# All weight matrices laid out by load on the host, one contiguous piece per partition

## What is computed

```python
def first_block(x, ...):
    p = rmsnorm(x) @ w_in                                  # 1024 x 4128
    y = concat(gated_delta_rule(...), mlstm(...))          # scans in both directions
    x = x + y @ w_out
    x = x + peer(rmsnorm(x), peer_wq, peer_keys, peer_u, peer_v)
    return rmsnorm(x)

def peer(t, ...):                                          # 256 tokens, 8 heads, 16 rows each
    idx, gate = top16_of(t @ peer_wq, peer_keys)           # row numbers below 16384
    act = gelu(einsum("td,thkd->thk", t, peer_u[idx]))     # 256 * 128 rows of 4 KB
    return einsum("thk,thkd->td", gate * act, peer_v[idx]) # as many again

def second_block(x, ctx, ada_w, pool_w, attn_w_qkv, attn_w_o, ffn_w_up, ffn_w_down, ...):
    # two layers: shift, scale and gate from ada_w (2 x 1024 x 6144); layer 0 mixes by
    # windowed means and pool_w, layer 1 by attention; each ends in
    #   (silu(a) * v) @ w_down   with   a, v = split(conv3(h @ w_up))   # 1024 x 5632, 2816 x 1024
    # layer 0 is also worked out for ctx (256 tokens), whose keys and values layer 1 reads
```

## Time and profile before

| what | us |
|---|---|
| median of 3 runs | 2010.51 |
| lowest and highest | 2008.73 and 2012.59 |
| the profiled execution | 2012.46 |
| its span | 2010.6 |
| PE / PEld / DVE busy | 1535.4 / 1126.8 / 1066.7 |
| ACT / POOL busy | 530.5 / 800.6 |
| DMA, mean | 237 GB/s, 475.83 MB |

### The profile page before, as it was taken

One profiled execution on the slowest core, in us unless ns is written; L12 is line 12 of the kernel. 1 busy time (PEld: TensorE's weight loads), 2 busy tenths in 40 slices (PEclk: granted clock), 3 DMA queues, 4 the chain that ended last, 5 costly groups with the idle time before them and its releaser, 6 DMA issues.

```text
span 2010.6 us, 22323 instructions
## 1 busy us (share of the span) xinstructions
PE 1535.4 (76%) x8566; PEld 1126.8 (56%) x8566; DVE 1066.7 (53%) x2051; ACT 530.5 (26%) x757; POOL 800.6 (40%) x750
## 2 busy tenths in 40 slices
PE   7958889797122849988787577775998968779988
PEld 6736556566111737754343111114998966569988
DVE  1353343439999887775666300016775334547743
ACT  3222211112221222210002000015654342546532
POOL 0004230007746446557777666642553001005530
PEclk9978999899555869989998799997999978889989
DMA  7322777239978789999999999961654421025531
GB/s 274 126 84 115 308 277 284 97 125 334 396 246 277 269 269 371 391 396 381 401 399 345 374 393 362 373 264 42 208 170 158 157 84 43 23 84 189 199 133 45
DMA packets 188138, 475.83 MB, mean 237 GB/s; under 512 B 10496, under 2 KB 80256, under 8 KB 184832
## 3 DMA queue, kind: packets, MB, share of 16 engines
q0 software_dynamic: 73728, 268.47, 35.7%
q1 hardware_dynamic: 114304, 205.93, 28.9%
HBM read 473.31 MB, written 1.05 MB: 236 GB/s over the span
## 4 chain that ended last, share of the span: by engine, by line
PE 30%; DVE 8%; DMA 8%; POOL 7%; issue 5%; ACT 3%; another core or an unknown queue 1%; DVEq 0%; ACTq 0%; POOLq 0%
PE ps L552 30%; POOL arena L2252 7%; DMA arena<-in_peer_v,cl 6%; DVE arena L1487 2%; DMA arena<-in_peer_u,arena 2%; DVE cvb L1175 1%; ACT sqb L1763 1%; DVE wl L1169 1%; ACT cvb L1763 1%; PE ps L556 0%; ACT L1763 0%; DVE st L1707 0%; DVE arena L1169 0%; ACT wh L1766 0%
## 5 line engine op out<-in xcount | busy, mean ns | idle before, releaser
L552 PE MATMUL ps<-arena,wring 128*128 128x256 f32 (+1 forms) x2848 | 697.2, 479 | 187.5 <-DMA arena<-in_peer_v,cl 78.3
L552 PEld LDWEIGHTS ps<-arena,wring 128*128 128x128 f32 (+1 forms) x2848 | 407.3, 167 | 473.2 <-DMA arena<-in_peer_v,cl 231.5
L2252 POOL DMA_INDIRECT arena<-in_peer_u,arena x256 | 306.4, 1197 | 243.7 <-DVE arena L1467 95.6
L1487 DVE CUSTOM_DVE_ANT_0 arena<-arena 128x1024 f32<-128x1024 f32 x256 | 305.3, 1223 | 94.5 <-DMA arena<-in_peer_u,arena 89.1
L2252 POOL DMA_INDIRECT arena<-in_peer_v,cl x256 | 262.3, 1024 | 172.5 <-PE ps L552 71.3
L1169 DVE TENSOR_TENSOR wl<-wring,wh 128x2048 fp32r<-128x2048 f32 x78 | 174.5, 2237 | 97.0 <-ACT wh L1766 95.0
L552 PE MATMUL ps<-hh,wh 128*128 128x256 f32 x704 | 203.5, 289 | 19.5 <-DVE hl L1169 13.9
L552 PE MATMUL ps<-hl,wh 128*128 128x256 f32 x704 | 202.2, 287 | 0.0
L552 PE MATMUL ps<-hh,wl 128*128 128x256 f32 x704 | 202.1, 287 | 0.0
L1763 ACT ACT_TABLE_LOAD x64 | 82.1, 1283 | 453.9 <-issue 135.0
L1169 DVE TENSOR_TENSOR arena<-arena,ps 128x512 f32<-128x512 f32 x64 | 43.8, 687 | 288.9 <-PE ps L552 283.0
(11 more groups left out here) (245 smaller groups left out, 1841.5 us busy)
## 6 DMA issues: line engine op xcount, KB each, us to landing
wring<-in_ffn_w_up SPq DMA_DIRECT2D x66, 1024.0 KB
wring<-in_ada SPq DMA_DIRECT2D x24, 2048.0 KB, 8.4
wring<-in_ffn_w_down SPq DMA_DIRECT2D x12, 2048.0 KB
wring<-in_w_in SPq DMA_DIRECT2D x8, 2048.0 KB, 13.9
wring<-in_ffn_w_down SPq DMA_DIRECT2D x6, 1536.0 KB
wring<-in_peer_wq SPq DMA_DIRECT2D x4, 2048.0 KB
wring<-in_attn_w_qkv SPq DMA_DIRECT2D x4, 2048.0 KB
wring<-in_w_out SPq DMA_DIRECT2D x2, 2048.0 KB
```

What stands on the lines that cost most here:

```text
L552: return pe.matmul(o, l, r, start=start, stop=stop)
L1487: ve.tensor_tensor_reduce(out=o, in0=o, in1=h2[:, t, :], scale=1.0, scalar=0.0, op0=MUL, op1=ADD, accum_out=dots[j % 2][:, k:k + 1]).then_ ...
L2252: po.indirect_dma_start(out=ring[:, n % NR, :], out_offset=None, in_=table, in_offset=bass.IndirectOffsetOnAxis(ap=which, axis=0)).then_in ...
```

## The change

Eight arrays are made on the host from the matrices, outside the timed execution: `in`, `wo`, `wq`, `qkv` and `ao` by `packed_cols`, `up`, `down` and `pool` by functions of their own. In each, what one load puts into one partition lies in one piece: 16 KB for a load of 2 MB, 12 KB for the shorter ones of `ffn_w_down`, 8 KB for `pool_w`. What a slot holds after a load, and at which place, is the same as before, and so are the order of the loads, the slots and what each load waits for. `ffn_w_up` now takes one DMA a load in place of two. The gathers are as they were. `down` has a row of 44 KB for each partition and half, of which a load reads a part.

```diff
+def packed_cols(w, starts):
+
+    w = np.transpose(np.reshape(w, (8, 128, -1)), (1, 0, 2))
+    return np.ascontiguousarray(np.stack([w[:, :, c:c + 512].reshape(128, 4096) for c in starts]))
+
+
+def packed_up(w):
+
+    w = np.reshape(w, (2, 8, 128, 2, 11, 256))
+    return np.ascontiguousarray(np.transpose(w, (0, 4, 2, 1, 3, 5)).reshape(22, 128, 4096))
+
+
+def packed_down(w):
+
+    w = np.reshape(w, (2, 22, 128, 2, 512))
+    return np.ascontiguousarray(np.transpose(w, (0, 3, 2, 1, 4)).reshape(4, 128, 11264))
+
+
+def packed_pool(w):
+    return np.ascontiguousarray(np.transpose(np.reshape(w, (8, 128, 256)), (1, 0, 2)).reshape(128, 2048))
+
+
...
-        def load(name, until, *parts, n=4):
+        def load(name, until, src, n=4):
 
             i = nth[0] % n
             nth[0] += 1
             if free[i]:
                 sp.wait_ge(*at(free[i][0], free[i][1]))
-            for put, src in parts:
-                sp.dma_start(put(slots[i]), src).then_inc(S[f"d_w{i}"], 16)
-                count[i] += 16
+            sp.dma_start(slots[i][:, 0:src.shape[1]], src).then_inc(S[f"d_w{i}"], 16)
+            count[i] += 16
             free[i] = until
             ready[name] = S[f"d_w{i}"], count[i], slots[i]
 
-        def kcols(w, c0, n):
-            return ((lambda ap: ap[:, 0:8 * n].rearrange("p (k c) -> p k c", k=8)),
-                    w[:, c0:c0 + n].rearrange("(k p) c -> p k c", p=128))
-
-        def pool_w():
-            return ((lambda ap: ap[:, 0:2048].rearrange("p (g c) -> p g c", g=8)),
-                    a["pool_w_2"][0].rearrange("g (k p) c -> p (g k) c", p=128))
-
-        def up_part(i):
-            return lambda ap: ap.rearrange("p (k i c) -> p k i c", k=8, i=2)[:, :, i, :]
-
-        def up(l, g):
-            w = a["ffn_w_up_2"][l]
-            return ((up_part(0), w[:, 256 * g:256 * g + 256].rearrange("(k p) c -> p k c", p=128)),
-                    (up_part(1), w[:, 2816 + 256 * g:3072 + 256 * g].rearrange("(k p) c -> p k c", p=128)))
-
         def down(l, half, f0, nf):
-            w = a["ffn_w_down_2"][l]
-            return ((lambda ap: ap[:, 0:512 * nf].rearrange("p (f c) -> p f c", f=nf)),
-                    w[128 * f0:128 * (f0 + nf), 512 * half:512 * half + 512].rearrange("(f p) c -> p f c", p=128))
+            return a["down"][2 * l + half][:, 512 * f0:512 * (f0 + nf)]
 
...
-        w_in = a["w_in"][0]
-        for n, c0 in enumerate((512, 1024, 0, 3088, 2064, 2576, 1536, 3600)):
-            load(("in", n), ("p_pj", 2 * n + 2), kcols(w_in, c0, 512))
+        for n in range(8):
+            load(("in", n), ("p_pj", 2 * n + 2), a["in"][n])
             if n == 2:
                 sp.dma_start(cl[:, :], a["c_levels"]).then_inc(S["d_l"], 16)
         for i in range(24):
-            load(("ada", i), ("p_ada", i + 1), (lambda ap: ap, a["ada"][i]))
+            load(("ada", i), ("p_ada", i + 1), a["ada"][i])
         for half in range(2):
-            load(("wo", half), ("p_wo", 2 * half + 2), kcols(a["w_out"][0], 512 * half, 512))
-        load(("wq", 0), ("p_q", 2), kcols(a["peer_wq"][0], 0, 512))
+            load(("wo", half), ("p_wo", 2 * half + 2), a["wo"][half])
+        load(("wq", 0), ("p_q", 2), a["wq"][0])
         nth[0] = 0
         sp.wait_ge(*at("g_lev", 28))
         sp.dma_start(g2b, a["norm2_g"][0].partition_broadcast(128)).then_inc(S["d_g2"], 16)
         sp.wait_ge(*at("p_hy", 4))
         sp.dma_start(flat(keyT), a["keys"]).then_inc(S["d_k"], 16)
         for q in range(1, 4):
-            load(("wq", q), ("p_q", 2 * q + 2), kcols(a["peer_wq"][0], 512 * q, 512), n=3)
+            load(("wq", q), ("p_q", 2 * q + 2), a["wq"][q], n=3)
         sp.wait_ge(*at("a_sc", 8))
         sp.dma_start(xin, a["ctx_2"][0].rearrange("(t p) d -> p t d", p=128)).then_inc(S["d_xc"], 16)
         sp.wait_ge(*at("v_h2", 2))
         sp.dma_start(cl[:, 0:1536], a["c_late"]).then_inc(S["d_l"], 16)
-        load("poolc", ("p_cpl", 4), pool_w(), n=3)
+        load("poolc", ("p_cpl", 4), a["pool"], n=3)
         for g in range(11):
-            load(("cup", g), ("p_cu", 2 * g + 2), *up(0, g), n=3)
+            load(("cup", g), ("p_cu", 2 * g + 2), a["up"][g], n=3)
         for half in range(2):
             for q, (f0, nf) in enumerate(((0, 8), (8, 8), (16, 6))):
                 load(("cdn", half, q), ("p_cd", 4 * (3 * half + q) + 4), down(0, half, f0, nf), n=3)
-        load("kvc", ("p_ckv", 3), kcols(a["attn_w_qkv_2"][0], 1024, 512), n=3)
+        load("kvc", ("p_ckv", 3), a["qkv"][2], n=3)
         nth[0] = 0
-        load("pool", ("p_pl", 4), pool_w(), n=3)
+        load("pool", ("p_pl", 4), a["pool"], n=3)
 
         def ffn_loads(l, n0):
             for g in range(11):
-                load(("up", l, g), ("v_lo", n0 + 2 * g + 2), *up(l, g), n=3)
+                load(("up", l, g), ("v_lo", n0 + 2 * g + 2), a["up"][11 * l + g], n=3)
             for half in range(2):
                 for q, (f0, nf) in enumerate(((0, 8), (8, 8), (16, 6))):
                     load(("dn", l, half, q), ("v_lo", n0 + 22 + 6 * half + 2 * q + 2), down(l, half, f0, nf), n=3)
 
         ffn_loads(0, 0)
-        load("kv", ("v_lo", 36), kcols(a["attn_w_qkv_2"][0], 1024, 512), n=3)
+        load("kv", ("v_lo", 36), a["qkv"][2], n=3)
         for q in range(2):
-            load(("q", q), ("v_lo", 38 + 2 * q), kcols(a["attn_w_qkv_2"][0], 512 * q, 512), n=3)
+            load(("q", q), ("v_lo", 38 + 2 * q), a["qkv"][q], n=3)
         for q in range(2):
-            load(("o", q), ("v_lo", 42 + 2 * q), kcols(a["attn_w_o_2"][0], 512 * q, 512), n=3)
+            load(("o", q), ("v_lo", 42 + 2 * q), a["ao"][q], n=3)
         ffn_loads(1, 44)
...
-_INS = ["x", "w_in", "w_out", "norm2_g", "peer_wq", "peer_u", "peer_v", "ctx_2", "pool_w_2", "attn_w_qkv_2",
-        "attn_w_o_2", "ffn_w_up_2", "ffn_w_down_2"]
+_INS = ["x", "norm2_g", "peer_u", "peer_v", "ctx_2"]
...
+    given |= {"in": packed_cols(x["w_in"][0], (512, 1024, 0, 3088, 2064, 2576, 1536, 3600)),
+              "wo": packed_cols(x["w_out"][0], (0, 512)), "wq": packed_cols(x["peer_wq"][0], (0, 512, 1024, 1536)),
+              "qkv": packed_cols(x["attn_w_qkv_2"][0], (0, 512, 1024)), "ao": packed_cols(x["attn_w_o_2"][0], (0, 512)),
+              "up": packed_up(x["ffn_w_up_2"]), "down": packed_down(x["ffn_w_down_2"]),
+              "pool": packed_pool(x["pool_w_2"][0])}
```

## The result

The changed kernel takes 2022.66 us (median of 5, 2016.69 to 2024.89), the kernel before 2010.18 us beside it on the same chip: ratio 1.0056, 95% interval 1.0037 to 1.0075. It is slower by 0.37 to 0.75%, more than the 0.2% that can be told from no change. The forecast was 2009.6 us, no change. The execution that was traced took 2016.69 us, the fastest of the five; its span is 2014.8 us. So the trace can show some 4 us of a loss whose median is 12 us, and the rest has to come from experiments. Read up to the start of the last gather it shows more, 1348.1 against 1338.8 us, 9.3 us; behind that point the traced execution of the changed kernel is 5.1 us shorter, 666.7 against 671.8 us.

The account below looks back on a forecast made before the run. Bounds by stage: TensorE up to 450 and from 1345 us, VectorE from 560 to 750, DMA engines (with TensorE to 900) otherwise. Sum +2 + (-1 + 2) - 2.6 - 1.3 = -0.9 us: 2009.6 us, no change; range 2000 to 2023 us.

Parts of the forecast that it names:

- the burst at 500 us: 500 to 560 us: pool_w and two ffn_w_up loads delay gathers, VectorE stalls; loss of 2 us, ends 0 and 4.7.
- 750 to 900 us: Loads among gathers, TensorE near its limit: -1 us for the saving, +2 us for stalls; ends -3.4 and +12.5.
- rival C: Lumps starve TensorE and VectorE of gathers, 12.5 us of it from 750 to 900 us: +11.9 us, 2022.4 us; chance 0.28.
- 900 to 1050 us: 3.8 loads of 2 KB pieces, DMA share 1.01, TensorE with time to spare: -2.6 us, ends 0 and -2.6.
- rival B: DMA engines bound 750 to 1200 us and the saving pays in full: -8.9 us, 2001.6 us, or 1998; chance 0.30.
- 1050 to 1200 us: pool_w and two ffn_w_up loads in one lump, half the 2.65 us saving used: -1.3 us, ends -2.65 and +3.
- Up to 450 us: w_in, w_out and peer_wq loads save engine time under TensorE's own work: 0, ends 0 and a gain of 1 us.
- 560 to 750 us: A burst of 6.7 us needs 2.7 of the ring's rows and gets 1; the ring covers that: 0.
- the last gathers and the end: 1200 to 1345 us, no load: 0; from 1345 us, 37 loads under TensorE's work: 0, at most 1 us gain.
- The saving per load: DMA engine time saved by long pieces: 1.06 us for a load of ffn_w_up, 0.69 us for one of the others.
- the second burst: pool_w and two ffn_w_up loads between 1050 and 1200 us: one lump of 17.5 us with 3 gathers; stage at -1.3 us.

Follow-up runs that it names:

- the long burst: pool_w and the first two ffn_w_up loads at 500 us in long pieces; alone, the other 19 loads among gathers in 2 KB pieces: 1.0063, 2027.11 us.
- the first pair: Changed kernel against the kernel before, on one chip, also called the first comparison: 2022.66 against 2010.18 us, ratio 1.0056.
- chip 2: Against the kernel before: changed kernel again 1.005; long pieces among gathers only in the 500 us burst 1.0063; 22 loads cut to an eighth 0.9911.
- the eighth of the bytes: Changed kernel with the 22 loads among the gathers cut to an eighth of their bytes: 0.9911 of the kernel before, 1995.85 us.
- second wait: Two ffn_w_up loads issued near 1122 us held until TensorE used 160 and 184 gathers; added alone to the changed kernel: 1.0012, 2000.56 us.
- chip 1: Against the kernel before: long only outside gathers 0.9995; long only in the 22 loads among gathers 1.0013; those 22 in 2 KB pieces 0.9991, 4 KB 0.9999.
- chip 3: Against the kernel before: 500 us burst in 2 KB pieces 1.0006, spread by waits 1.0004, both bursts spread 0.9975; all 22 loads in 2 KB 1.0015.
- chip 4: Against the kernel before: both waits on the old layout 1.0001; changed kernel with later wait alone 1.0012, without waits 1.0014, with both 0.9981.

## Why the prediction was wrong

*The step that failed is the burst at 500 us.* I forecast -0.9 us, no change, and the kernel got slower. The mechanism was right in each part: turns piece for piece, a load that passes one or two gathers, VectorE with no time to make up. The size was not. I took 2 us between ends of 0 and 4.7 us, by supposing that up to seven of the ring's ten rows would have landed. The ring ran empty in all six traces with the long burst, and 4.5 to 8.0 us were lost (75.4 to 78.7 us against 70.7 to 70.9 us; one trace of the kernel before has 72.4 us). I had read a full ring out of the 41 waits of GpSimd for VectorE; those say that the slots are taken, not that their data is there. That `poolc`, first in the burst, used up part of the reserve is likely, and no run took it out alone. The gains that were to outweigh the burst, -1, -2.6 and -1.3 us, did not come in the first pair either: from gather 64 to 400 it shows +3.9 us in their place.

*Small slips in the working.* Rows 8 count 144 packets a gather, so beside a load of 1 KB pieces 14 gathers pass in 24 us, not 16 in 27 us. The 33 gathers from 500 to 560 us are GpSimd's issues; VectorE used 31, one in 1.94 us. Rows 12 don't show the two loads of `ffn_w_up` issued within 2 us: in the kernel before their four DMAs keep SyncE issuing from 499.40 to 543.35 us, and only the changed kernel issues both within 1.03 us. None of these moves the burst's 2 us by much.

*The runs lose more than the traces show.* In the first comparison and on chip 2 the medians lose 8.9 to 12.5 us. The traced executions, each the lowest of its set, lie 4.0, 6.5 and 8.8 us above the median of the kernel before. Part of the difference lies behind the last gather: from its start to the end these three take 666.7 to 668.2 us, where the two traces of the kernel before take 671.8 and 671.5 us. All 18 traces lie between 666.4 and 674.5 us there, those with the old layout in that stage at 669.4 to 671.8 us, so the layout doesn't sort them, and a short end can hide some 4 us of the loss. How long the ends of the untraced executions are isn't on record. That the rest hangs on the same burst is likely, since 1.0050 to 1.0063 with it stands against 1.0004 and 1.0006 without it, but these are different chips. Why the loss is 0.5 to 0.6% on two comparisons with slower chips and 0.13 and 0.14% on the faster ones stays open.

*750 to 900 us.* I took -1 us for the saving and +2 us for stalls, with rival C's 12.5 us as the other end. TensorE's waits there:

```profile
PE ps L558 <- DVE wt L1177: 30.6, 1, 30.6
PE ps L554 <- DVE arena L1171: 10.0, 1, 10.0
PE ps L554 <- DMA arena<-in_peer_v,cl: 2.2, 5, 1.3
```

Gathers ended 2.2 us, 3.4 us before: neither a gain nor a stall of note. (The 30.6 us began before 750 us and ended just behind it; the kernel before has 29.9 us ending just ahead of it.) So rival C had the sign and the mechanism but the wrong place. That its 2022.4 us are so near the measured 2022.66 us is luck, since 12.5 us of its sum came from this stage. It looked where seven loads come one by one, and one load at a time the ring covers; the price comes where three come together and the consumer has no slack. A load beside gathers now moves 1.39 MB in 4 us, so 2.097 MB in 6.0 us, close to the 6.7 us that I worked out; the queues from 802 to 806 us:

```profile
q1 hardware_dynamic: 85, 1.39, 81.9%
q0 software_dynamic: 88, 0.34, 20.9%
```

*900 to 1050 us.* I took the whole 2.6 us, because the DMA share was 1.01. The share fell to 0.97 and nothing got shorter: gathers 64-256 take 394 to 400 us in every layout with whole loads. So rival B, which has the saving paid in full, doesn't hold, and the eighth of the bytes paid a fifth to a quarter. A DMA share of 1.01 had looked like a bound, and was one only in part. What else holds the pace there no run took apart; how far ahead the ring lets GpSimd go is a candidate.

*1050 to 1200 us.* I took -1.3 us, ends -2.65 and +3. It came in the form that I gave it, in one lump and given back, and the part given back is smaller: gathers 256-383 take 194.8 to 198.4 us in the three traces with all pieces of 1 KB there and 200.1 to 205.1 us in the ten with 2 KB and more and no second wait, and the 17 gathers behind them 28.9 to 29.9 us against 21.7 to 26.9 us. In the first pair that is +6.1 and -4.8 us, +1.3 us, inside the ends; on chip 1 it is 222.5 against 224.1 us, -1.6 us, and on chip 2 225.8 against 227.3 us, -1.5 us, close to what I took. What decides isn't 16 KB against 1 KB alone, since 2 KB does the same.

*Up to 450 us, 560 to 750 us, the last gathers and the end.* Taken at 0, and measured at 0 within 0.2%: 0.9995 with the long pieces there alone. (From 560 to 750 us that run has the old layout; this stretch rests on the time of gathers 64-256.)

*The saving per load.* Alone and in pieces of 16 KB the loads of `ffn_w_up` ran, from 1400 to 1500 us,

```profile
q1 hardware_dynamic: 1157, 16.78, 46.2%
```

at 363 GB/s, 5.77 us a load, where I had 5.45 us from those of `ada`: a saving of 0.74 us in place of 1.06 us. It changes little, since next to nothing of the saving is paid.

With the measured sizes (the burst 4.5 to 8.0 us, the savings up to 1050 us at 0, the second burst at +1.3 us) the sum is +6 to +9 us, 2016 to 2020 us. The first pair's traces have +9.3 us at the last gather. The median is 2022.66 us, and what remains is not explained.

## What to carry to other kernels

Where two DMA queues take turns piece for piece, the length of a piece sets who gets the engines: longer pieces for the loads save DMA time and take it from a stream of gathers beside them. Before lengthening them, find the places where several loads are issued at once, and ask there how many gathers have landed, not how many were issued, and whether their consumer has time to spare. A DMA share of 1.0 doesn't say that DMA time saved is time saved: cutting the loads to an eighth for one run tells what it is worth.

## What the runs showed of the hardware

Between the two queues the counts stay at about one piece for one, whether the load's pieces have 1 KB beside the gathers' 4 KB (931 gather packets to 932), 4 KB (594 to 597) or 16 KB (88 to 85 within a load, and 308 to 241 over the burst). The Trainium skill, page "DMA: Bandwidth & Descriptors", section "Queues, rings and completion order", has an engine go round the queues packet by packet, with up to 64 descriptors to a packet; the going round agrees, and the counts fit a grain of one piece: in 4 us, when each engine moved some five pieces of 16 KB, as many gather packets went by.

Chips differ by more than the change does. The kernel before takes 1996.77 and 1997.61 us on two of them, 2010.18, 2012.65 and 2014.66 us on the others. Nearly all of that is in gathers 400-511, 142 to 144 us against 158 to 160 us in the traces without loads there. GpSimd's waits from 1200 to 1345 us, of the changed kernel on a slower chip, then on a faster one:

```profile
POOL arena L2254 <- remote: 19.1, 9, 3.3
```

```profile
POOL arena L2254 <- issue: 22.3, 73, 0.3
POOL arena L2254 <- PE ps L554: 11.5, 25, 0.5
```

On the slower one GpSimd stands still nine times for up to 3.3 us, for something that isn't in this core's records, and the kernel before does so seven times. On the faster ones there is no such wait. The gathers themselves are slower there, too: from 1210 to 1325 us they take 97.5% of the engines' time for 42.19 MB on the slower chip and 102.5% for 47.02 MB on the faster one, 6% more time for the same bytes. What is behind both stays open. Two loads moved into this stretch cost 2.9 us on chip 3 and 10.1 us on chip 4 (161.6 against 158.7 us, 152.2 against 142.1 us); that the pauses leave room for them on chip 3 is a guess, which no run tested.
